# Retention of eight heads, taken in four pairs instead of one head at a time, with the diagonal factor of the decay added before the exponential

## What is computed

```
scores[s, t] = k_s . q_t                                  (contraction over 64)
decay[s, t]  = exp(lg_f * max(t - s, 0) + lg_b * max(s - t, 0)) * (2 if s == t else 1)
o_t          = sum_s scores[s, t] * decay[s, t] * v_s     (contraction over 256)
             + state_f^T (q_t * qdecay_f) + state_b^T (q_t * qdecay_b)   (contraction over 64)
```

## Time and profile before

| | us |
|---|---|
| median of 3 runs (1962.14 to 1965.26) | 1963.5 |
| the profiled execution | 1962.31 |
| its span, first to last instruction | 1960.5 |
| outside the span | 1.8 |
| mean granted TensorE clock | 0.941 of 2.4 GHz |

### The profile page before, as it was taken

One profiled execution on the slowest core, in us unless ns is written; L12 is line 12 of the kernel. 1 busy time (PEld: TensorE's weight loads), 2 busy tenths in 40 slices (PEclk: granted clock), 3 DMA queues, 4 the chain that ended last, 5 costly groups with the idle time before them and its releaser, 6 DMA issues.

```text
span 1960.5 us, 32359 instructions
## 1 busy us (share of the span) xinstructions
PE 1747.7 (89%) x12088; PEld 1588.0 (81%) x12088; DVE 1231.2 (63%) x2112; ACT 862.2 (44%) x1272; POOL 168.1 (9%) x167
## 2 busy tenths in 40 slices
PE   7899998899979968498796357999999999999997
PEld 1898978899979857497686356899999999999997
DVE  1657456677544467741549989666666666666665
ACT  2424444566454357120342179444444444444443
POOL 0000010022000001140017610000000000000000
PEclk9999999999989979796798689999999999999999
DMA  8666304555535412100232100455555555555553
GB/s 322 228 229 245 108 22 152 181 181 184 181 108 182 141 65 67 41 1 1 86 129 87 65 1 0 147 179 188 193 183 183 190 192 179 185 193 186 181 190 118
DMA packets 38520, 278.92 MB, mean 142 GB/s; under 512 B 4400, under 2 KB 4528, under 8 KB 5040
## 3 DMA queue, kind: packets, MB, share of 16 engines
q1 hardware_dynamic: 35136, 254.82, 38.0%
q0 software_dynamic: 2304, 16.78, 2.2%
q10 hardware_dynamic: 1008, 6.30, 0.9%
HBM read 276.83 MB, written 1.05 MB: 142 GB/s over the span
## 4 chain that ended last, share of the span: by engine, by line
PE 78%; DVE 13%; ACT 6%; issue 2%; DMA 1%; POOL 1%; ACTq 0%; SPq 0%; DVEq 0%; POOLq 0%
PE ps L421 78%; DVE piece L1392 1%; DMA ring<-in_stream 1%; ACT small L1331 1%; DVE arena L1855 1%; DVE arena L1847 1%; DVE arena L1849 1%; DVE arena L1844 1%; DVE arena L1852 1%; ACT piece L994 1%; DVE arena L1693 1%; DVE arena L1877 1%; ACT small L1338 0%; DVE arena L1864 0%; DVE arena L1766 0%
## 5 line engine op out<-in xcount | busy, mean ns | idle before, releaser
L421 PEld LDWEIGHTS ps<-h_r,piece 128*128 128x128 f32 x6384 | 801.8, 195 | 63.0 <-issue 49.5
L421 PE MATMUL ps<-h_r,piece 128*128 128x256 f32 x6384 | 811.6, 287 | 45.1 <-POOL piece L397 20.5
L1392 DVE TENSOR_TENSOR piece<-ring,piece 128x1024 fp32r<-128x1024 f32 x448 | 554.8, 1244 | 325.2 <-ACT piece L994 323.0
L994 ACT ACTIVATE piece<-ring 128x1024 fp32r<-128x1024 f32 x464 | 487.1, 1056 | 437.1 <-PE ps L421 425.3
L421 PE MATMUL ps<-piece,late_r 128*128 128x512 f32 x1536 | 372.4, 391 | 1.5 <-DVE late_r L1923 1.5
L421 PEld LDWEIGHTS ps<-piece,late_r 128*128 128x128 f32 x1536 | 280.3, 188 | 54.7 <-DVE late_r L1923 1.7
L1918 DVE TENSOR_TENSOR late<-late,arena 128x256 f32<-128x256 f32 x128 | 81.5, 637 | 132.6 <-ACT late L1354 132.6
L421 PE MATMUL ps<-arena 128*64 128x128 f32 (+8 forms) x696 | 124.9, 375 | 28.9 <-DVE arena L1726 8.7
L1354 ACT ACTIVATE late<-ps 128x256 f32<-128x256 f32 x128 | 49.3, 385 | 224.1 <-PE ps L421 224.0
L421 PEld LDWEIGHTS ps<-arena 128*128 128x128 f32 (+4 forms) x696 | 93.3, 203 | 56.2 <-issue 14.5
L421 PE MATMUL ps<-ffn_hi,piece 128*128 128x256 f32 x352 | 63.5, 283 | 0.8 <-DVE piece L1392 0.8
(11 more groups left out here) (289 smaller groups left out, 1839.9 us busy)
## 6 DMA issues: line engine op xcount, KB each, us to landing
ring<-in_stream SPq DMA_DIRECT2D x240, 1024.0 KB, 4.9
arena<-in_mod POOLq DMA_DIRECT2D x16, 1024.0 KB, 5.9
arena<-in_const ACTq DMA_DIRECT2D x1, 2256.0 KB, 8.8
arena<-in_const ACTq DMA_DIRECT2D x1, 1888.0 KB, 9.2
xres<-in_xT SPq DMA_DIRECT2D x1, 1024.0 KB, 10.5
arena<-in_xT SPq DMA_DIRECT2D x1, 1024.0 KB, 12.6
arena<-in_subk ACTq DMA_DIRECT2D x1, 1024.0 KB, 5.1
out<-arena SPq DMA_DIRECT2D x2, 512.0 KB, 2.7
```

Of the source, the lines that this page charges most:

```text
L421: mm_last[0] = nc.tensor.matmul(*args, **kw)
L994: A(piece[:, 0, c % 3], ring[:, p % RING, s], ACT.Copy).then_inc(S["hi_ready"], 1)
L1392: TT(piece[:, 1, c % 3], ring[:, p % RING, s], piece[:, 0, c % 3].bitcast(F32), ALU.subtract).then_inc(S["lo_ready"], 1)
```

## The change

Scores and outputs are issued in pairs of heads. Within a pair the 64-row matmuls alternate between an even head (partitions 0 to 63) and an odd one (64 to 127); the 128-row matmuls stay one after the other. `probs` gets four buffers at another place. The constant `mask12` becomes `ln2_same` (ln 2 on the diagonal, 0 elsewhere) and is added by DVE in the first instruction of `decay_arg`, which becomes a tensor by scalar plus tensor; POOL's eight multiplications and the semaphore `decay_m` go. ACT's list is as it was.

```diff
--- before.py
+++ after.py
@@ -62,7 +62,7 @@
 
 
 CONST1 = [("cosq", 256), ("sinq", 256), ("cosk", 256), ("sink", 256), ("dist_f", 512), ("dist_b", 512),
-          ("mask12", 512), ("dft_d", 256), ("dft_l", 1024), ("perm", 128), ("pos_ctx", 32), ("pos_q", 512)]
+          ("ln2_same", 512), ("dft_d", 256), ("dft_l", 1024), ("perm", 128), ("pos_ctx", 32), ("pos_q", 512)]
 
 CONST2 = [("mask4", 512), ("m1", 128), ("m1t", 128), ("levels", 640), ("scan", 256), ("causal", 512), ("sel", 512),
           ("wa_up", 512), ("g_up", 512), ("w_if", 64)]
@@ -82,7 +82,7 @@
 CP, NP_ = widths(PCONST)
 
 SEMS = """acc_free0 acc_free1 x_in mod_used lo_ready fin_out out_dma c_silu stat1 mod2_step mod2_mm const1_in
- decay_exp decay_m ffn_ready gelu_done gated gated_hi x_new mqk_pad bon_in w_exp rk_ready const2_in gram_sb
+ decay_exp ffn_ready gelu_done gated gated_hi x_new mqk_pad bon_in w_exp rk_ready const2_in gram_sb
  p1_mm mt_ready places place_no placed hi_ready g_mm selt_sb piece_used acc_ready hn_mm hn_sq hn_sqmm
  xs_sq xs_mm mrow_sb pconst_in sq1 mod_cols h_ready perm_mm kw_ready state_mm qk_ready probs scores o_sb out_mm
  state_sb qdec fourier1 four_sb fourier2 z_sb rows_done uc_mm bc_mm mqk_silu uc_sb m_probs ms_mm em_row m_h
@@ -172,7 +172,7 @@
         fT = w3(24064, 4)
         oT = w3(25088, 8)
         decay = w3(27136, 2, 512)
-        probs = w3(28160, 2, 512)
+        probs = w3(0, 4, 512)
         qdec = w3(29184, 8)
         st_f = at(31232, 512)
         st_b = at(31744, 512)
@@ -330,11 +330,6 @@
                 pool.wait_ge(S["mod2_step"], n - 1)
                 mod_page(n % 2, n)
 
-            pool.wait_ge(S["const1_in"], 16)
-            for hh in range(8):
-                pool.wait_ge(S["decay_exp"], hh + 1)
-                g.tensor_tensor(decay[:, hh % 2], decay[:, hh % 2], c1("mask12"), ALU.mult).then_inc(S["decay_m"], 1)
-
             g.engine_nop().then_inc(S["ffn_ready"], 2)
 
             def gated_page(u, i=0):
@@ -602,36 +597,42 @@
                 fm_page(PAGE["bg"] + u, TURN["bg"] + u, h)
 
 
-            def scores(n):
-                r, j = (n % 2) * 64, n // 2
-                if n >= 2:
-                    pe.wait_ge(S["probs"], n - 1)
+            def scores(m):
+                if m:
+                    pe.wait_ge(S["probs"], 2 * m)
                 for st in range(2):
-                    m = mm(ps[:, 4 + n % 2, st * L:(st + 1) * L], qk[r:r + 64, 4 + j, st * P:(st + 1) * P],
-                           qk[r:r + 64, j, :], start=True, stop=True)
-                m.then_inc(S["scores"], 1)
-
-            def outputs(n):
-                r, j = (n % 2) * 64, n // 2
-                pe.wait_ge(S["probs"], n + 1)
-                if n >= 2:
-                    pe.wait_ge(S["o_sb"], n - 1)
-                o = ps[:, 6 + n % 2, 0:L]
-                for st in range(2):
-                    mm(o, v_tok[:, st, n * P:(n + 1) * P], probs[:, n % 2, st * L:(st + 1) * L], start=st == 0,
-                       stop=False)
-                mm(o, st_f[r:r + 64, j * P:(j + 1) * P], qdec[r:r + 64, j, :], start=False, stop=False)
-                mm(o, st_b[r:r + 64, j * P:(j + 1) * P], qdec[r:r + 64, 4 + j, :], start=False,
-                   stop=True).then_inc(S["out_mm"], 1)
+                    for e in range(2):
+                        r = 64 * e
+                        s_ = mm(ps[:, 4 + e, st * L:(st + 1) * L], qk[r:r + 64, 4 + m, st * P:(st + 1) * P],
+                                qk[r:r + 64, m, :], start=True, stop=True)
+                        if st == 1:
+                            s_.then_inc(S["scores"], 1)
+
+            def outputs(m):
+                pe.wait_ge(S["probs"], 2 * m + 2)
+                if m:
+                    pe.wait_ge(S["o_sb"], 2 * m)
+                for e in range(2):
+                    n = 2 * m + e
+                    for st in range(2):
+                        mm(ps[:, 6 + e, 0:L], v_tok[:, st, n * P:(n + 1) * P], probs[:, n % 4, st * L:(st + 1) * L],
+                           start=st == 0, stop=False)
+                for d, st_ in enumerate((st_f, st_b)):
+                    for e in range(2):
+                        r = 64 * e
+                        o = mm(ps[:, 6 + e, 0:L], st_[r:r + 64, m * P:(m + 1) * P], qdec[r:r + 64, 4 * d + m, :], start=False,
+                               stop=d == 1)
+                        if d == 1:
+                            o.then_inc(S["out_mm"], 1)
 
             pe.wait_ge(S["qk_ready"], 4)
             scores(0)
             pe.wait_ge(S["state_sb"], 2)
             pe.wait_ge(S["qdec"], 2)
-            for n in range(8):
-                if n < 7:
-                    scores(n + 1)
-                outputs(n)
+            for m in range(4):
+                if m < 3:
+                    scores(m + 1)
+                outputs(m)
 
 
             for n in range(8):
@@ -1540,7 +1541,7 @@
 
             def decay_arg(n):
                 d = decay[:, n % 2, :]
-                dv(TS(d, c1("dist_f"), lgrow[:, n:n + 1], None, ALU.mult))
+                dv(STT(d, c1("dist_f"), lgrow[:, n:n + 1], c1("ln2_same"), ALU.mult, ALU.add))
                 STT(d, c1("dist_b"), lgrow[:, 8 + n:9 + n], d, ALU.mult, ALU.add).then_inc(S["decay_arg"], 1)
 
             def bg_page(u):
@@ -1556,10 +1557,10 @@
                     decay_arg(u - 4)
             for n in range(8):
                 dve.wait_ge(S["scores"], n + 1)
-                dve.wait_ge(S["decay_m"], n + 1)
-                if n >= 2:
-                    dve.wait_ge(S["out_mm"], n - 1)
-                TT(probs[:, n % 2, :], ps[:, 4 + n % 2, :], decay[:, n % 2, :], ALU.mult).then_inc(S["probs"], 1)
+                dve.wait_ge(S["decay_exp"], n + 1)
+                if n >= 4:
+                    dve.wait_ge(S["out_mm"], n - 3)
+                TT(probs[:, n % 4, :], ps[:, 4 + n % 2, :], decay[:, n % 2, :], ALU.mult).then_inc(S["probs"], 1)
                 if n < 6:
                     dve.wait_ge(S["probs"], n + 1)
                     decay_arg(n + 2)
@@ -2033,7 +2034,7 @@
         sel[n, n] = 1
     pos_ctx = np.stack([np.stack([255 - k] * 8 + [k] * 8, axis=1) for k in key.T], axis=1)
     k1 = {"cosq": cos / 8, "sinq": sin / 8, "cosk": cos, "sink": sin, "dist_f": np.maximum(dist, 0),
-          "dist_b": np.maximum(-dist, 0), "mask12": 1 + (dist == 0),
+          "dist_b": np.maximum(-dist, 0), "ln2_same": np.log(2.0) * (dist == 0),
           "dft_d": np.concatenate([np.cos(dn), np.sin(dn)], axis=1) * scale, "dft_l": dft_l,
           "perm": (q[:, None] == (q[None, :] ^ 32)), "pos_ctx": pos_ctx,
           "pos_q": np.broadcast_to(np.concatenate([s + 1, 256 - s])[None], (P, 512))}
```

## The result

The change makes the kernel slower, by under 1%: 1985.04 us median of 6 runs (1978.67 to 1987.26) against 1964.34 of 6 (1962.14 to 1973.43), ratio 1.0086 with a 95% interval of 1.0067 to 1.0105. The profiled execution took 1985.0 us, span 1983.2. The page's chain keeps its shape (PE 78%, DVE 13%, ACT 5%); PE's mean granted clock fell from 0.941 to 0.931.

What follows compares the result with a forecast made beforehand. The prediction took PE to bound the kernel (busy 89% of the span, 78% of the chain). One execution's 1962.31 us plus 5.7 for the serial chain and 7.1 for the clock gave 1975 us, range 1968 to 1981.

Steps and rivals of the forecast that it cites:

- Direction and mechanism: Retention: slower, chance 0.91; ACT's exponentials wait for outputs, so pairs run serially and PE's stops lower its clock.
- R: Retention window, from PE's first score weight load to its first Fourier weight load; 25.2 us in the kernel before.
- The serial chain: Retention: PE, ACT and DVE work one after another for each pair, costing 5.7 us at an unchanged clock.
- The turns of 8.04: Retention: from one pair's second product to the next pair's, 8.04 us where two heads took 5.96.
- Overlap of the halves: PE's 64-row matmuls: opposite halves run at the same time, sparing 6.0 us over all heads.
- The price of the exponent: DVE in the retention: the first exponent instruction goes from 0.47 to 0.75 us, line 1544's form from 1.83 to 0.75.
- The clock: PE in the retention: slow bursts behind four idle stretches cost 7.1 us, bounds 0 and about 15.
- The starting point: Whole kernel: the terms were added to one profiled execution, 1962.31 us, 1.2 us under the median shown.
- (a): Rival, retention: engines still overlap and DVE's 4.34 us a pair is the limit; 1958.0 us, chance 0.05.
- (b): Rival, retention: pairs serial, but PE's clock holds at 1.00; 1968.0 us, chance 0.12.
- (e): Rival, PE: alternating calls don't overlap, 6.0 us more; 1974 with held clock or 1980 with lowered clock, chance 0.08.
- (d): Rival, retention: nearly every PE burst runs at 1.2 GHz, 15 us for the clock; 1983 us, chance 0.05.

Runs made afterwards that it cites:

- e1_exp_first: The changed kernel with ACT's exponentials for the next pair moved before its waits for this pair's outputs: R 24.0 us, ratio 0.9992 to the kernel before.
- e2_keep_busy: The changed kernel, order untouched, with useless fp32 matmuls filling PE's idle stretches (the filled kernel): R 30.6 us, ratio 1.0007 to the kernel before.
- e9_early_exponents: e5_four_decays with the four early exponents one page earlier and their exponentials before ACT's page 5: R 20.7 us, ratio 0.9971 to the kernel before.
- e10_output_banks: e9_early_exponents with pair 2's outputs in PSUM banks 2 and 3: R 19.8 us, 1961.57 us median, ratio 0.9962 to the kernel before.
- e5_four_decays: The changed kernel with four buffers of decay, exponents and exponentials reordered, exponentials before ACT's output waits: R 23.6 us, ratio 0.9979 to the kernel before.
- e8_heads_four_decays: e5_four_decays with PE taking one head at a time, as in the kernel before: R 46.9 us, ratio 1.0125 to the kernel before.
- e11_heads_early: e9_early_exponents with PE taking one head at a time, as in the kernel before: R 24.8 us, ratio 0.9997 to the kernel before.
- e7_half_busy: The changed kernel with about half of PE's idle time filled by useless matmuls: R 33.9 us, ratio 1.0050 to the kernel before.

## Why the prediction was right and wrong, by its steps

- **Direction and mechanism: right.** ACT's exponentials behind the output waits make the pairs serial (e1_exp_first takes 17 us out of R with that edit alone), and PE's stops lower the clock (e2_keep_busy).
- **The serial chain: right.** Predicted 5.7 us at an unchanged clock; the filled kernel has 30.57 - 25.23 = 5.3. The turns of 8.04 measured 8.08 and 8.06, the last ones of 6.77 and 2.98 measured 6.68 and 2.99; only the start was 0.3 us shorter.
- **Overlap of the halves: right**, 0.73 us for eight loads wherever the clock was high. That the alternation is not needed for it was not foreseen.
- **The price of the exponent: right**, 0.75 us for both instructions and no row at 1.8.
- **The clock: wrong in size.** The step was "each of the three long stretches costs 1.7 to 2.6, I take 2.1 (6.3), and the 2.7 us one nothing or 1.7, I take 0.8. Sum of the clock 7.1 us". Measured: 2.8, 2.5 and 2.3 for the three and 2.7 for the last, 10.4 together. The lengths of the stops were right: by the ends of the matmuls, in which the prediction counted, they were 3.71, 3.96, 3.94 and 2.56 us for its 3.96, 3.9, 3.9 and 2.7. Their price was not. It was averaged over a row with a short and a row with a long spell at 1.2 GHz; here all four were long, 27 us of 41, and the shortest stop cost as much as the longer ones. The row with 3.0 us idle and no loss, taken as a sign of mercy, had no counterpart in the changed kernel. What decides whether a stop is followed by a long spell, a short one or none is open.
- **The Trainium skill** ("TensorE: Matmul & The Clock Gate", section "Why this matters for your kernels") warns of idle gaps between bursts of matmuls, but of longer ones than the last stop by the ends of the matmuls, 2.56 us. That stop was paid in full all the same, so here the measurement decides.
- **The starting point: too low, and the larger part of the miss.** R was forecast at 25.2 + 12.8 = 38.0 and is 41.0; that alone would have given 1978, inside the range. The other 6.9 us of the way from 1975 to 1985 lie outside the retention. The step was to add the change to one execution: "The profiled execution lies 1.2 us under the median shown, which is inside the spread of the three runs, so I leave it". That execution had 1935.3 us outside R, the least of the fourteen profiles, whose median is 1941.0; from that median the forecast R gives 1980.8 and the measured one 1983.8. Three runs of before didn't show how far it varies; later ones went from 1962 to 1974. That these 6.9 us have nothing to do with the change is likely, but not shown.
- **A match by luck.** When it ran again the change was 0.62% slower than before, 12 us, 1978.8 in the median, which is close to the forecast. R was 41.2 in that run's profile too, so the sizes were no better there; the spread of the rest went the other way. The 15.7 us of R, 0.80%, lie in both intervals of the ratio.
- **Rivals.** (a) was not what ran, yet its premise, exponentials out of the way, makes e9_early_exponents and e10_output_banks faster than before. (b) is out, the clock did not hold, and so is (e), the calls overlap. (d), given 0.05, is out by its price, 10.4 us and not 15, but not by far in what it says: the clock came back only for the last 1.1 to 1.6 us of three bursts and not at all in the fourth. That its time, 1983, is near the measured one is chance: its 15 us stand where 10.4 of clock and most of the 6.9 outside R were.

## What to carry to other kernels

When work is grouped to please one engine, look at the lists of the others for a step that stood behind a single unit's result and now stands behind the whole group's: two units half a turn apart had hidden it, one group can't. Price the stops that this opens on TensorE twice: for the time that the serial chain adds, 5.3 us here, and for the slow bursts behind them, 10.4 us. When rows of like stops give different prices, give the sum for the dearest of them too, and let the range reach it. And before a change of some microseconds is added to one execution, see how far several executions of the same kernel lie apart.

## What the runs showed of the hardware

- **A clock that does not come back.** With the same lists and a stop of 4 us or so, pairs of heads were back at 2.4 GHz within the first burst (e5_four_decays, 0.86 over R), while one head at a time stayed at 1.2 GHz for 42.3 us with PE busy throughout (e8_heads_four_decays, 0.50) and came back some 4 us into the Fourier matmuls behind (0.50 until 288.0, 0.83 over the next two microseconds). With a stop of 1.96 us the same order kept 1.00 (e11_heads_early). The two orders differ in how the 64-row matmuls stand on PE: pairs have both halves at work at once, one head at a time has one half. Whether that or something else kept the clock low is open; no run tested it.
- **Halves overlap by what is queued.** Two calls in one half followed by two in the other ran at the same time as well as alternating ones: 16 loads in 1.70 and 1.60 us.
- **The same work, another clock.** With PE busy for 39.8 and 39.9 of 40 us, the clock of the stretch from 120 to 160 was 1.00 in one execution and 0.91 in another, on a stretch of PE's list that the change leaves alone. In the second the low clock lay between 134 and 142, where PE had been busy without a gap for over ten microseconds.
- **Stops of 2 us.** In this stretch the clock held behind stops of 1.50, 1.56 and 1.70 us by the ends of the matmuls (the kernel before, e11_heads_early, e7_half_busy) and fell around those of 2.02, 2.03 and 2.25 (e7_half_busy, e9_early_exponents). It is no rule for other places: behind a stop of 3.0 us it stayed at 1.00 elsewhere in the kernel before.
